# A transformer kernel on one core: the first slab behind each adaptive norm computed from h times the feature scale and fixed in its bank afterwards

## What is computed

```
mod = silu(c) @ w_ada + b_ada
sh1, sc1, g1, sh2, sc2, g2 = split(mod, 6)

h = rmsnorm(x, norm1_g) * (1.0 + sc1) + sh1
proj = h @ w_in                      # q, k, v and the pool branch: attention, pooling mixer
x = x + g1 * (concat([att, pool]) @ w_out)

h2 = rmsnorm(x, norm2_g) * (1.0 + sc2) + sh2
x = x + g2 * conv_gated_ffn(h2, w_up, conv_w, conv_b, w_down)
```

## Time and profile before

| | us |
|---|---|
| median of 3 runs (1394.36 to 1400.7) | 1395.54 |
| the profiled execution | 1396.78 |
| its span | 1394.9 |
| PE busy | 1359.2 (97% of the span) |
| DVE / ACT / POOL busy | 660.9 / 620.2 / 614.2 |
| TensorE's wide products of L1365 to L1367 | some 0.39 each by their records, overlapping |

### The profile page before, as it was taken

The page is one execution under the profiler, slowest core; times in us unless marked ns, Lnnn a source line. Parts: engine busy times, 40 slices in busy tenths (PEclk is TensorE's granted clock), DMA queues, the critical chain, the costliest instruction groups (busy, mean ns, idle before and its releaser), DMA issues.

```text
span 1394.9 us, 17281 instructions
## 1 busy us (share of the span) xinstructions
PE 1359.2 (97%) x6530; PEld 1091.9 (78%) x6530; DVE 660.9 (47%) x976; ACT 620.2 (44%) x862; POOL 614.2 (44%) x448
## 2 busy tenths in 40 slices
PE   9999999999999999999999999988999999999999
PEld 7877955788876888888888887854878888888887
DVE  5434948256433454334343316588255455554111
ACT  5555228553444443434442214688245545554211
POOL 3444320374440456555564544411336555555453
PEclk9999999999999999999999999999999999999999
DMA  7223111143220244344446533200312222323422
GB/s 268 91 90 110 71 57 65 60 157 117 91 91 1 91 139 147 135 151 146 148 142 247 190 130 111 91 31 31 122 61 90 90 93 91 117 90 136 178 94 91
DMA packets 29215, 155.23 MB, mean 111 GB/s; under 512 B 3056, under 2 KB 4464, under 8 KB 14960
## 3 DMA queue, kind: packets, MB, share of 16 engines
q1 hardware_dynamic: 29168, 154.57, 31.0%
HBM read 152.46 MB, written 2.10 MB: 111 GB/s over the span
## 4 chain that ended last, share of the span: by engine, by line
issue 39%; PE 30%; POOL 26%; DVE 4%; DMA 0%; POOLq 0%; SPq 0%; ACT 0%
POOL wlo L385 26%; PE lin L1365 10%; PE lin L1366 10%; PE lin L1367 10%; DVE small L1023 1%; DVE expd L1034 1%; DMA raw<-w_slabs 0%; PE lin L1574 0%; PE c_act L1421 0%; DVE xl L902 0%; DVE win L1242 0%; DVE small L1027 0%; POOLq L394 0%; PE att L1436 0%; DVE wlo L909 0%
## 5 line engine op out<-in xcount | busy, mean ns | idle before, releaser
L385 POOL TENSOR_TENSOR wlo<-raw,whi 128x512 fp32r<-128x512 f32 x444 | 614.0, 1415 | 765.3 <-ACT whi L412 506.2
L1365 PE MATMUL lin<-xh,whi 128*128 128x512 f32 x1072 | 420.6, 392 | 4.3 <-POOL wlo L385 3.5
L1367 PE MATMUL lin<-xh,wlo 128*128 128x512 f32 x1072 | 417.3, 389 | 0.0
L1366 PE MATMUL lin<-xl,whi 128*128 128x512 f32 x1072 | 417.2, 389 | 0.0
L412 ACT ACTIVATE whi<-raw 128x2048 fp32r<-128x2048 f32 x66 | 126.6, 1919 | 265.9 <-PE lin L1367 260.4
L1365 PEld LDWEIGHTS lin<-xh,whi 128*128 128x128 f32 x1072 | 201.2, 188 | 53.3 <-issue 6.2
L1367 PEld LDWEIGHTS lin<-xh,wlo 128*128 128x128 f32 x1072 | 201.2, 188 | 42.2
L1366 PEld LDWEIGHTS lin<-xl,whi 128*128 128x128 f32 x1072 | 201.3, 188 | 41.4 <-issue 0.5
L1365 PE MATMUL lin<-fh,whi 128*128 128x512 f32 x352 | 137.0, 389 | 0.0
L1367 PE MATMUL lin<-fh,wlo 128*128 128x512 f32 x352 | 136.9, 389 | 0.0
L1366 PE MATMUL lin<-fl,whi 128*128 128x512 f32 x352 | 136.9, 389 | 0.0
(11 more groups left out here) (320 smaller groups left out, 1918.0 us busy)
## 6 DMA issues: line engine op xcount, KB each, us to landing
raw<-w_slabs SPq DMA_DIRECT2D x111, 1024.0 KB, 4.8
...
```

Of the source, the lines that this page charges most:

```text
L385: return nc.gpsimd.tensor_tensor(wlo[s][:, ks, :], raw[s][:, ks, :], f(whi[s][:, ks, :]), ALU.subtract)
L1365: nc.tensor.matmul(out, whi_, xhi_, start=first, stop=False)
L1366: nc.tensor.matmul(out, whi_, xlo_, start=False, stop=False)
L1367: return nc.tensor.matmul(out, wlo_, xhi_, start=False, stop=last)
```

## The change

For each adaptive norm the first slab's products no longer take the normalised tiles. The norm is a factor per token (one over the root) and the shift a summand per feature, so W(h * gain / root + shift) is (W(h * gain)) / root + W shift. `scaled_slab` on TensorE multiplies the weights with h * gain, split in two parts (`sch`, `scl`), and beside them, with two columns, with the shift, split as well (`shift_hl`), into columns 8 and 9 of `att[0]` and `att[3]`: two narrow products for each step and half, 32 in a slab. The eight norm sums (now in `att[2]`) stand in steps 2 and 3, the four broadcast products in steps 4 to 6. The filler products are gone.

ScalarE makes `sch` (`scaled_hi`) and VectorE `scl` (`scaled_lo`) beside the products of `down` and `out2`; ScalarE and VectorE split the shift there. At norm1 they lie in `xh` and `xl` themselves, so the normalised tile k may only be written when the scaled slab has read it (`scaled["read"]`); at norm2 they have memory of their own. The diagonals are now made on ScalarE, which also copies the broadcast bank with the factor D into `rstd`; VectorE's tiles are h * gain * `rstd`. Behind VectorE's tile 5 and the low part of tile 4 stands `fix_slab`: with the scaled slab done, it sums the two columns of the shift, multiplies both banks by `rstd` and adds the shift's sum. Who reads those banks waits for `scaled["fixed"]`. `make_hi(g + 2)` stands in `finish_norm` between tiles 2 and 3 (before: in2's behind `pool_in`, ffn2's in the loop), and the first turn of ffn2's loop is written out, with `make_hi(ffn2 + 3)` behind the middle taps of slab 1. The second slab takes its steps as the normalised tiles come.

```diff
@@ ScalarE
-            def finish_norm(n, hi, shift, beside):
+            def finish_norm(n, hi, shift, g):
+                make_hi(g + 1)
                 act.wait_ge(n["sum"], 1)
-                nc.scalar.activation(token_root, att[0][:, 0:TT], ACT.Sqrt, bias=ccol(C_EPS)).then_inc(n["sd"], 1)
-                beside()
+                nc.scalar.activation(token_root, att[2][:, 0:TT], ACT.Sqrt, bias=ccol(C_EPS)).then_inc(n["sd"], 1)
+                act.wait_ge(n["sd"], 2)
+                for t in range(TT):
+                    nc.scalar.activation(tmp[0][:, P * t:P * (t + 1)], ident, ACT.Copy, scale=token_root[:, t:t + 1]
+                                         ).then_inc(n["inv"], 1)
+                act.wait_ge(n["sum"], 2)
+                nc.scalar.activation(rstd[:, :], att[1][:, :], ACT.Copy, scale=float(D)).then_inc(n["sd"], 1)
                 for k in range(KT):
+                    if k == 3:
+                        make_hi(g + 2)
+                    if n is norms["norm1"]:
+                        act.wait_ge(scaled["read"], k + 1)
                     act.wait_ge(n["x"], k + 1)
...
             pool_in(0, 0)
-            make_hi(SLAB0["in2"] + 2)
...
+            act.wait_ge(scaled["fixed"], 4)
+            for s in range(2):
+                convolve(0, s)
+                if s:
+                    make_hi(SLAB0["ffn2"] + 3)
+                gated_hi(0, s, fh[:, s, :])
+            with act.Fori(1, FT // 2) as i:
@@ VectorE
+            def scaled_lo(i, u):
+                for k in range(2 * u, 2 * u + 2):
+                    dve.wait_ge(scaled["hi"], KT * i + k + 1)
+                    nc.vector.scalar_tensor_tensor(scl[i][:, k, :], h[:, k, :], gain(i, k), f(sch[i][:, k, :]),
+                                                   ALU.mult, ALU.subtract).then_inc(scaled["lo"], 1)
+            def fix_slab(i, p):
+                dve.wait_ge(slab_done, SLAB0["in2" if i == 0 else "ffn2"] + 1)
+                for j in range(2):
+                    nc.vector.tensor_reduce(slab_shift[i][:, j:j + 1], att[3 * j][:, 8:10], AX.X, ALU.add)
+                banks = lin[2 * (p % 2):2 * (p % 2) + 2]
+                for b in banks:
+                    last = nc.vector.tensor_tensor(b[:, :], b[:, :], rstd[:, :], ALU.mult)
+                link(last)
+                for j, b in enumerate(banks):
+                    nc.vector.tensor_scalar(b[:, :], b[:, :], slab_shift[i][:, j:j + 1], None, ALU.add
+                                            ).then_inc(scaled["fixed"], 1)
...
-                    nc.vector.scalar_tensor_tensor(tmp[k % 4][:, :], h[:, k, :], gain(k), att[1][:, :],
+                    nc.vector.scalar_tensor_tensor(tmp[k % 4][:, :], h[:, k, :], gain(i, k), rstd[:, :],
                                                    ALU.mult, ALU.mult).then_inc(n["x"], 1)
                     if k >= 1:
                         low(k - 1)
+                    if k == 5:
+                        fix_slab(i, p)
                 low(KT - 1)
@@ TensorE
+                for k in range(KT):
+                    pe.wait_ge(scaled["lo"], KT * i + k + 1)
+                    for j in range(2):
...
+                        nc.tensor.matmul(out, wh, sch[i][:, k, :], start=(k == 0), stop=False)
+                        nc.tensor.matmul(out, wh, scl[i][:, k, :], start=False, stop=False)
+                        nc.tensor.matmul(add, wh, shift_hl[i][:, k, :], start=(k == 0), stop=False)
+                        mm = nc.tensor.matmul(out, wl, sch[i][:, k, :], start=False, stop=(k == KT - 1))
...
+                        mm = nc.tensor.matmul(add, wl, shift_hl[i][:, k, :], start=False, stop=(k == KT - 1))
...
+                        t = 2 * (k - 2) + j
+                        if 0 <= t < TT:
+                            for e, (part, made, count) in enumerate(((rstd, n["acc"], 4), (tmp[3], n["sq"], KT))):
+                                pe.wait_ge(made, count)
+                                mm = nc.tensor.matmul(att[2][:, t:t + 1], part[:, P * t:P * (t + 1)], ccol(C_MEAN_D),
+                                                      start=(e == 0), stop=(e == 1))
...
+                        t = 2 * (k - 4) + j - 1
+                        if 0 <= t < TT:
+                            pe.wait_ge(n["inv"], t + 1)
+                            mm = nc.tensor.matmul(att[1][:, P * t:P * (t + 1)], mean_d, tmp[0][:, P * t:P * (t + 1)],
+                                                  start=True, stop=True)
```

162 lines of the change are left out of this document (99 added, 63 removed).

## The result

The changed kernel took 1409.3 us (median of five runs, 1407.98 to 1410.52) where the kernel before took 1398.94 beside it: a ratio of 1.0085, 95% interval 1.0073 to 1.0097, so some 12 us slower (the two medians taken alone are 10.4 apart). The profiled execution took 1408.81, span 1406.9, against a span of 1394.9 before: 12.0 us more.

The account below looks back on a forecast made before the run. TensorE, busy 97% of the span, was taken as the bound. Terms 5.5 (in2), 1.7 (clock) and 6.1 (ffn2) sum to 13.3 us; 1396.78 + 13.3 = 1410.1 profiled, median 1408.8 us; eight-in-ten range 1398.0 to 1415.5.

Parts of the forecast that it names:

- in2's fourth slab: Behind norm 1: GpSimd's low part ready at 894.5, so this slab starts 5.5 us later, after a 4 us TensorE wait.
- ffn2: Behind norm 2: third slab 3.8 us late for its bank, fourth slab 6.1 us late for GpSimd's low part.
- VectorE's chain: VectorE's tiles and low parts at each norm, fix and waits included: last low part ends about X + 16.
- X: Start of VectorE's first normalised tile at each norm: forecast t0 + 15.3, against t0 + 6.0 in the kernel before.
- The first slab: First slab behind each norm: ends at t0 + 17.2, 3.8 us earlier than before at norm 1, 3.2 at norm 2.
- t0: Time at which the follower of the last product ahead of a norm would start on TensorE: 845.01 and 1020.65.
- The two-column product: In the first slab: 0.11 us each, 3.5 us for 32; the cited 25 ns floor would give 0.8 us.
- the contention with GpSimd: In VectorE's chain: operations beside GpSimd's 5.9 us of work, around tiles 3 to 5, cost 0.3 us more together.
- The rule of the Trainium skill cited there: VectorE instructions with two SBUF inputs contend with GpSimd, those with at most one don't; worth about 0.4 us per norm.
- The second slab: Behind each norm: ends at t0 + 33.3, 1.4 and 2.0 us late, TensorE waiting some 3 us at step 5.
- The clock: Granted clock falls behind the 4 us wait in in2; charged once at 1.7 us, bounds 0 and 5.
- only the first slabs count: Rival: VectorE and ScalarE keep ahead of the second slab, only the shorter gap counts: -7.0 us, 1388.5, chance 0.10.

Follow-up runs that it names:

- e4: Changed kernel without 28 of the 32 two-column products of each scaled slab, only the last step's left; ratio 1.0035 to the kernel before.
- e11: e10 with the high part of slab g+2 made ahead of tile 5 instead of tile 3; ratio 0.9977 to the kernel before.
- e9: Changed kernel with the 32 two-column products of each first slab issued behind its wide products, none removed; ratio 1.0046 to the kernel before.
- e7: Changed kernel with VectorE's normalised tiles reading the broadcast root in its bank instead of ScalarE's SBUF copy; ratio 1.0044 to the kernel before.
- e12: Changed kernel with only the high part of slab g+2 made ahead of tile 5 instead of tile 3, both norms; ratio 1.0056 to the kernel before.
- e2: Changed kernel with the high part of slab in2+3 made right behind ScalarE's copy of the first slab's banks; ratio 1.0054 to the kernel before.
- e5: Changed kernel with the fix of the first slab's bank moved from behind tile 5 to behind the last low part; ratio 1.0090 to the kernel before.
- e1: Kernel before with only ScalarE's first turn of the ffn2 loop written out; 1394.86 against 1396.89 us, ratio 0.9987.
- e10: e7 with the edits of e2 and e9 added; ratio 1.0015 to the kernel before.

## Why the prediction was right

The forecast was 1408.8 us and the measurement 1409.3; forecast and measured difference of the executions are 13.3 and 12.0. That the absolute numbers meet within 0.5 us is luck in part: the kernel before, at 1395.54 in the runs behind the forecast, took 1398.94 beside the changed one, and the misses below have both signs (+0.9 at in2's fourth slab, -0.3 at ffn2's, -1.9 behind it). The mechanism was right: the normalised tiles come later, VectorE's chain is longer, and ScalarE's and GpSimd's order passes that on. Step by step, with X for the start of VectorE's first normalised tile as in the prediction:

- **The first slab.** Expected end t0 + 17.2, measured: the last two-column product starts at t0 + 17.2. The two-column product: 0.11 taken, 0.106 to 0.113 by e4 and 0.11 in the rows of e11. By the floor of 25 ns of the Trainium skill that is cited with it, the first slab was estimated 2.7 us shorter. The rows show why the floor is not the cost here: the product behind a two-column one does start only 0.03 later (845.66, 845.69), but then takes 0.32 instead of 0.23 to its own follower (846.01).
- **X.** Expected t0 + 15.3, measured 15.4. That the change pays with this lateness is shown by e4, and by e9 for as far as ScalarE's order lets it.
- **VectorE's chain.** Expected X + 16, measured X + 17.3. This sum has the mis-sized terms: the bare 16 operations 11.3 instead of 12.0, the fix 2.78 instead of 3.2, the wait for slab g+2's high part 0.62 instead of 0.6, and **the contention with GpSimd 2.6 instead of 0.3** (0.54, 1.03 and 1.01 on three operations). The step that failed reads the surcharge of a low part behind a bank reader and takes it for that of any operation with two SBUF inputs; where two of them follow each other, each pays 1.0. e7 and e12 show it. The rule of the Trainium skill cited there pointed in the right direction, and its weight was put at 0.4 per norm instead of 1.7 (1.03 and 0.63 in e7). The price stood in the trace of the kernel before, only in another place: the windows behind norm 1 have two SBUF inputs and follow one another, and four of them lay under GpSimd's low part of 869.20 to 875.87, at 1.7 to 1.8 each instead of 0.7.

```profile
869.50 1.80 DVE L1237 TENSOR_TENSOR win<-upool 128x527 f32<-128x527 f32 x1
871.33 1.68 DVE L1242 TENSOR_TENSOR win<-win 128x525 f32<-128x525 f32 x1
```

- **The second slab.** Expected end t0 + 33.3, measured 34.75 at norm 1. The single wait of 3 us at step 5 was four waits, 5.4 in all, the longest 2.45 behind the fix.
- **in2's fourth slab.** +5.5 expected, +6.4 measured, by the chain that was named: copy, windows, roundings, squares, high part, GpSimd. From the end of VectorE's chain to GpSimd's end it took 17.6 us; the forecast's terms for it add up to 17.7, but its text goes on with 894.5 where they give 894.1. TensorE's wait of 4 us was 3.25, since the third slab was later too. e2 shows that the order on ScalarE is the cause.
- **ffn2.** +3.8 and +6.1 expected, +4.95 and +5.8 measured. The third slab waits for the bank's readers; e5 shows that reader as TensorE's wait. That the fourth comes out near the forecast although the chain ends 1.2 us later is luck: the gating of slab 0 behind the third tap, charged with some 5 us and a table load in it, took 3.0 (1064.41 to 1067.39), as the load now runs beside VectorE's taps. (The forecast's own terms add up to about 1069.5 and not to its 1069.0.)

```profile
1062.98 1.28 ACT L867 ACT_TABLE_LOAD   x1
```

- **The clock.** +1.7 once, measured 1.6 once in the profile, at the place named. It also fell to 0.57 behind norm 2's last wait, where the wait for the bank hides it. In other executions it fell elsewhere: it is not as steady as the other terms.
- **What was missed.** "From there the loop has its old order and runs at 10.9 a slab" is wrong: the loop of the kernel before ran at 10.98 a slab because of two table loads a turn, and the changed one at 10.88. That is -1.9 in the trace and -2.2 in e1. Without it the difference would have been 13.9 us, 0.6 above the forecast; with it the difference is 1.3 below.

The rival "only the first slabs count" named its own turning point, X = t0 + 13.9 without the fix and the high part; with X at t0 + 12.2 to 12.9 in e9 and e10 and both of them still there, the gain was not had, and e11, with the high part out of the way, came down to the kernel before. So the rival's condition was of the right kind.
